# RWKV's chunk stage on 64x64 corners of TensorE, and heads in pairs in retention's scores and in the low-rank step

## The chip, the cores and the metric

The kernel runs on one core of a Trainium2 chip. The metric is device time in microseconds (us), the median of three runs. TensorE (PE in the profile) has two granted clocks, 1.2 and 2.4 GHz; the profile gives the granted clock as a share of the higher one.

## The reference, cut to what matters

A two-layer first block is followed by a second block of two layers with four attention variants, which the change does not touch. Each layer of the first block normalises `x` (256 tokens x 1024), projects it to retention, forgetting-attention and RWKV columns and to gates, runs the three branches (4 heads of 64 each), merges them and runs a gated FFN. The change is in three places: the RWKV recurrence, retention's scores, and RWKV's low-rank products.

```python
def step(state, ...):                       # one token, per head, state 64 x 64
    sa = jnp.einsum('bhvk,bhk->bhv', state, a_t)
    state = (state * w_t[:, :, None, :] + sa[..., None] * b_t[:, :, None, :]
             + v_t[..., None] * k_t[:, :, None, :])
    return state, jnp.einsum('bhvk,bhk->bhv', state, r_t)
...
w_pre = -jax.nn.softplus(-(w0 + jnp.tanh(xw) @ w2)) - 0.5    # xw: 64 columns
a = jax.nn.sigmoid(a0 + xa @ a2)                             # xa: 64 columns
g = jax.nn.sigmoid(xg) @ g2                                  # xg: 128 columns
```

The kernel computes the recurrence in chunks of 64 tokens. Within a chunk it needs the products of `a`, `r`, `b` and `k` of all token pairs, masked to the lower triangle, and the inverse of a unit triangular 64x64 matrix, which it builds in five doubling levels. From that follow each chunk's contribution to the state and to the output.

## The kernel before, in words

All matmuls write fp32 into eight PSUM banks of 128 partitions x 512. Banks 0 to 3 belong to the big projections, banks 4 to 7 to the branches. The weights of the projections come in pieces of 1 MB into a ring (SyncE's queue), ScalarE (ACT) makes a rounded high part (L1309), VectorE (DVE) the low part (L1710), and PE multiplies the parts in three fp32r passes.

PE's program is written out by hand (L1019 to L1107). From L1039 on, the gate columns are projected in 48 small units, `fill` (L649): each is 12 matmuls of 128x128 weights and 256 columns, all on line L659, and four of them make one group of 256 columns. The units stand between the pieces of the branches, so that PE has work while DVE or ACT handle a branch's last result. In the chunk stage (L1068 to L1102) the 256 tokens are two tiles `t` of 128 tokens, two chunks in each. Per tile PE runs:

- `rt_transposes` (L823): 16 transposes, of 64 columns each, so that head features lie in rows 0 to 63.
- `rt_matrices` (L846): per head, products over those 64 rows (L850, L851), 128 tokens by 256; then L855.
- levels v = 1 to 5: `rt_level_p` (L858), four 128x128 products (one a head, L865), then DVE's mask L2003; `rt_level_q` (L868), eight such products (L872, L873; only the four of L873 at v = 5), then DVE's two adds L2008 and L2009. One `fill` unit follows each P and each Q (none the last Q).
- `rt_ak_v` (L876, L878), `rt_solve` (L882, L886), `rt_chunk_terms` (L889: L892, L896, L901, L902), `rt_state` (L905: L912), `rt_output` (L916: L922, L923, L925, L926).

A 128x128 matrix of a tile holds the two 64x64 matrices of its chunks on its diagonal; the other half is masked to zero. An fp32 matmul leaves two records of each kind in the trace (two weight loads, two matmuls: I call them passes), an fp32r matmul or a transpose one.

DVE runs, in the levels of a tile, the masks and adds and between them whole jobs of 2048 columns in the table `slots`: a low part (L1710) or a scaling of gates (L1964). GpSimd copies chunk operands into zero-padded tiles (L2309, L2310) for L896, L901 and L902.

Retention (before the chunk stage) transposes q and k one head at a time (L682), ACT copies them, and `ret_scores` (L685) makes per head a product of 256 and one of 128 columns (L690, L691) over rows 0 to 63. The low-rank step transposes its 256 columns in three parts (L796 to L798) and multiplies by three weights (L806), two of them 64 rows high and both in rows 0 to 63.

Of the kernel before, what the change touches and what calls it, by code (L numbers as in the profile page):

```python
# [23 lines left out]
P = 128  # L24
D = 1024
KT = D // P
S = 256
# [42 lines left out]
def constant_tables():  # L70
# [15 lines left out]
    strict, incl = same * (j < i[None]), same * (j <= i[None])  # L86
    t["rmask"] = np.concatenate([strict, incl, strict, incl], 1)
    lev = []
    for l in range(LEVELS):
        s = 1 << l  # L90
        lev.append((j // (2 * s) == i[None] // (2 * s)) & (j // s % 2 == 1) & (i[None] // s % 2 == 0))
    t["lev0t"] = lev[0].T
# [81 lines left out]
def build(nc, x_in, w_in, w_fox, lora_w, p_all, w_out, w_gate_up, w_down, cols, vec1, mu, w_in2, w_out2,  # L174
          vec2, rpb, tables, out):
    with ExitStack() as ctx:
# [17 lines left out]
        lora = sb("lora", [P, 3, W4])  # L194
# [115 lines left out]
        ret_tp = sig("ret_tp", 4)  # L310
        ret_qk = sig("ret_qk", 4)
# [54 lines left out]
        rt_tp = sig("rt_tp", 8)  # L366
        rt_T = sig("rt_T", 8)
        rt_mat = sig("rt_mat", 8)
        rt_msk = sig("rt_msk", 8)
        rt_a = sig("rt_a", 2)  # L370
        rt_t0 = sig("rt_t0", 2)
# [8 lines left out]
        rt_zz = sig("rt_zz", 2)  # L380
        rt_vz = sig("rt_vz", 2)
        rt_rq = sig("rt_rq", 2)
        rt_rqc = sig("rt_rqc", 2)
        rt_g = sig("rt_g", 2)
        rt_gc = sig("rt_gc", 2)
# [3 lines left out]
        rt_sm = sig("rt_sm", 2)  # L389
        rt_y = sig("rt_y", 2)  # L390
# [49 lines left out]
        r_qk = carve(5120, 2048)[0]  # L440
        r_st, r_c = carve(0, 1536, 512)
        r_qkT = r_qk.rearrange("p (a h s) -> p a h s", a=2, h=NH)
# [12 lines left out]
        mats = scratch[:, 0:2048].rearrange("p (h c) -> p h c", h=NH)  # L455
        lo, w_ex, w_t1, w_t2 = carve(0, 512, 512, 512, 512)
        m_t, m_tt, m_p = (a.rearrange("p (h c) -> p h c", h=NH) for a in carve(2048, 512, 512, 512))
# [4 lines left out]
        m_g = carve(4096, 512)[0].rearrange("p (h c) -> p h c", h=NH)  # L462
        w_b = carve(4096, 512)[0]
        m_h = carve(4608, 512)[0].rearrange("p (h c v) -> p h c v", h=NH, c=2)
        w_kk = carve(4608, 512)[0]
        m_art = carve(5120, 1024)[0].rearrange("p (h c) -> p h c", h=NH)
        w_lT = carve(5120, 768)[0].rearrange("p (a s) -> p a s", a=3)
        m_bT, m_kT = (a.rearrange("p (h c) -> p h c", h=NH) for a in carve(6144, 512, 512))
# [4 lines left out]
        w_x = carve(8704, 1024)[0].rearrange("p (t h c) -> p t h c", t=NT, h=NH)  # L473
        w_bt, w_kt = carve(9728, 512, 512)
        m_s = carve(10752, 768)[0].rearrange("p (n h v) -> p n h v", n=3, h=NH)
        w_y, w_c2 = carve(11520, 512, 256)
        w_f3 = st[:, 424:488]
        w_fs = w_f3[:, 0:32].rearrange("p (n h c) -> p n h c", n=NT, h=NH)
        w_fe = w_f3[:, 32:44].rearrange("p (n h) -> p n h", n=3)

        kept = sb("kept", [P, 2560])
        m_zz, m_bz, m_vz = (kept[:, i * 512:(i + 1) * 512].rearrange("p (h c v) -> p h c v", h=NH, c=2) for i in range(3))
        m_rq = kept[0:HD, 1536:2560].rearrange("p (h c s) -> p h c s", h=NH, c=2)
# [32 lines left out]
        def _(sp):  # L516
# [16 lines left out]
            for l in range(DEPTH):  # L533
                ll = slice(l, l + 1)
                for n in range(len(IN_STARTS)):
# [4 lines left out]
                    if n == 3:  # L540
                        sp.dma_start(vec[:, 0:N_VEC1], vec1[ll].broadcast_to([P, N_VEC1])).then_inc(vec_in.sem, 16)
                        for i, k in enumerate((HD, HD, P)):
                            sp.dma_start(lora[0:k, i, :], lora_w[ll, i, 0:k, :].rearrange("o k n -> (o k) n"))\
                                .then_inc(lora_in.sem, 16)
                        sp.dma_start(w_mu, mu[ll].broadcast_to([P, 1024])).then_inc(mu_in.sem, 16)
# [48 lines left out]
        def _(pe):  # L594
# [77 lines left out]
            def ret_transposes(l):  # L672
# [5 lines left out]
                for a in range(2):  # L678
                    for t in range(NT):
                        for h in range(NH):  # L680
                            c = a * W4 + h * HD
                            last = tp(bank[4 + 2 * a + t][0:HD, h * P:(h + 1) * P], r_rot[:, t, c:c + HD], ident)  # L682
                        last.then_inc(ret_tp.sem, 1)

            def ret_scores(l):  # L685

                pe.wait_ge(*ret_qk.after(l, 4))
# [103 lines left out]
            def rw_lora_transposes(l):  # L791
                pe.wait_ge(*rl_s.after(l, 1))
                pe.sem_inc(passed.sem, 1)
                for t in range(NT):
                    s = lo[:, t * W4:(t + 1) * W4]
                    tp(bank[4][0:HD, t * P:(t + 1) * P], s[:, 0:HD], ident)  # L796
                    tp(bank[4][0:HD, S + t * P:S + (t + 1) * P], s[:, HD:2 * HD], ident)
# [3 lines left out]
            def rw_lora_products(l):  # L801
                pe.wait_ge(*rl_T.after(l, 1))
                pe.wait_ge(*lora_in.after(l, 3))
                for i, k in enumerate((HD, HD, P)):
                    for t in range(NT):
                        last = mm(bank[6 + i if i < 2 else 4][:, t * W4:(t + 1) * W4], w_lT[0:k, i, t * P:(t + 1) * P],  # L806
                                  lora[0:k, i, :], start=True, stop=True)
                    last.then_inc(rl_mm.sem, 1)

            def rw_decay_sums(l):  # L810
# [5 lines left out]
                for t in range(NT):  # L816
                    for h in range(NH):
                        c = (t * NH + h) * 4
                        last = mm(bank[6][0:HD, c:c + 4], w_lw[:, t * W4 + h * HD:t * W4 + (h + 1) * HD], tab["sel"],
                                  start=True, stop=True)  # L820
# [1586 lines left out]
```

## Time and profile before

| | |
|---|---|
| median of three runs (lowest to highest) | 1258.4 us (1252.48 to 1261.07) |
| the profiled execution: its time, its span | 1258.48 us, 1256.7 us |
| PE busy | 1223.0 us, 97% of the span |
| PE weight loads / DVE / ACT / GpSimd busy | 89% / 60% / 39% / 5% |
| mean granted clock | 0.99 |

A row of the timeline gives start, duration, engine, line, operation, tiles, shape and count. Shapes are rows*columns of the weights, then rows x columns of the moving operand. Matmuls overlap in their tails, so the cost of one to the engine is the distance from its start to the next start, not its duration; "x8" is eight records in a row of which the row gives the start of the first and the end of the last.

### The profile page before, as it was taken

To read this page: it belongs to the slowest core of one execution; us is meant where nothing else is said; L and a number is where in the kernel's file an instruction comes from. 1 tells how busy PE (TensorE), PEld (TensorE's weight loads), DVE (VectorE), ACT (ScalarE), POOL (GpSimd) and SP (SyncE) were. 2 spreads that over 40 slices of the span, in tenths; PEclk is the share of its full clock that TensorE was granted. 3 is DMA by queue.
4 is the path that set the end of the run, shared out by engine and by line. 5 is a ranking of instruction groups with operands and counts; after the bars stand their busy time and mean duration, and the time that the engine had idled before them with its cause. 6 is when DMAs were issued, how large, how long until landed. Compare 5 with 4: busy or idle time off the path is not lost. (4 is left out here: it accounts for less than half of the span.)

```text
span 1256.7 us, 19719 instructions
## 1 busy us (share of the span) xinstructions
PE 1223.0 (97%) x8388; PEld 1118.9 (89%) x8388; DVE 754.0 (60%) x942; ACT 495.8 (39%) x686; POOL 61.9 (5%) x67
## 2 busy tenths in 40 slices
PE   4999999999999999999999999999999999999997
PEld 3789999989999999789999989999999788887886
DVE  4486656465655556586647464655567765566654
ACT  3355412124333335355413113333335564455642
POOL 0002001000000000002001000000000300011000
PEclk9999999999999999999999999999999999999999
DMA  7643312425554445342222425544443534254320
GB/s 296 226 139 128 103 68 76 193 101 201 201 201 176 165 160 213 117 163 102 101 68 100 168 101 202 201 192 164 164 180 134 206 132 166 106 182 154 106 101 34
DMA packets 27458, 188.25 MB, mean 150 GB/s; under 512 B 3457, under 2 KB 4353, under 8 KB 5505
## 3 DMA queue, kind: packets, MB, share of 16 engines
q1 hardware_dynamic: 25808, 175.89, 37.9%
q10 hardware_dynamic: 1440, 8.55, 1.7%
q0 software_dynamic: 144, 2.89, 0.6%
q8 instruction: 48, 0.79, 0.3%
q14 instruction: 18, 0.14, 0.0%
HBM read 182.07 MB, written 5.24 MB: 149 GB/s over the span
## 5 line engine op out<-in xcount | busy, mean ns | idle before, releaser
L634 PE MATMUL bank<-in_low,h_high 128*128 128x512 f32 x352 | 139.7, 397 | 0.0
L634 PE MATMUL bank<-in_high,h_high 128*128 128x512 f32 x288 | 118.7, 412 | 19.3 <-DVE in_low L1710 18.6
L1710 DVE TENSOR_TENSOR in_low<-ring,in_high 128x2048 fp32r<-128x2048 f32 x48 | 109.9, 2295 | 34.4 <-ACT in_high L1309 34.4
L982 PE MATMUL bank<-h_high,gate_split 128*128 128x256 f32 x704 | 129.2, 281 | 0.2
L982 PE MATMUL bank<-h_high,up_split 128*128 128x256 f32 x704 | 128.8, 281 | 0.0
L1309 ACT ACTIVATE in_high<-ring 128x2048 fp32r<-128x2048 f32 x48 | 91.3, 1909 | 68.4 <-PE bank L634 68.0
L998 PE MATMUL bank<-act_split,down_split 128*128 128x256 f32 x960 | 118.2, 283 | 0.0
L998 PEld LDWEIGHTS bank<-act_split,down_split 128*128 128x128 f32 x960 | 116.4, 191 | 0.0
L659 PE MATMUL bank<-h_high,in_high 128*128 128x256 f32 x384 | 116.0, 302 | 0.5 <-DVE in_low L1710 0.5
L634 PE MATMUL bank<-in_high,x_low 128*128 128x512 f32 x288 | 114.3, 397 | 0.0
L982 PEld LDWEIGHTS bank<-h_high,gate_split 128*128 128x128 f32 x704 | 110.4, 189 | 0.9 <-DVE h_low L1661 0.6
L982 PEld LDWEIGHTS bank<-h_high,up_split 128*128 128x128 f32 x704 | 110.3, 189 | 0.0
L659 PE MATMUL bank<-x_low,in_high 128*128 128x256 f32 x384 | 109.4, 285 | 0.0
L659 PE MATMUL bank<-h_high,in_low 128*128 128x256 f32 x384 | 109.2, 284 | 0.0
L982 PE MATMUL bank<-h_low,up_split 128*128 128x256 f32 x352 | 99.4, 282 | 0.0
L982 PE MATMUL bank<-h_low,gate_split 128*128 128x256 f32 x352 | 99.3, 282 | 0.0
L634 PEld LDWEIGHTS bank<-in_high,h_high 128*128 128x128 f32 x288 | 55.3, 192 | 31.0 <-issue 18.9
L1483 ACT ACTIVATE gate_split<-ring 128x2048 fp32r<-128x2048 f32 x24 | 46.0, 1916 | 91.6 <-PE bank L982 72.5
L634 PEld LDWEIGHTS bank<-in_low,h_high 128*128 128x128 f32 x352 | 67.4, 192 | 13.6 <-issue 0.5
L659 PEld LDWEIGHTS bank<-h_high,in_high 128*128 128x128 f32 x384 | 74.5, 194 | 2.3 <-DVE in_low L1710 1.0
L1335 ACT ACTIVATE arena<-bank 128x512 f32<-128x512 f32 x24 | 14.3, 597 | 156.7 <-PE bank L659 156.7
L2082 DVE TENSOR_TENSOR down_split<-ring,down_split 128x2048 fp32r<-128x2048 f32 x20 | 45.8, 2292 | 49.8 <-ACT down_split L1483 49.8
(326 smaller groups left out, 2503.3 us busy)
## 6 DMA issues: line engine op xcount, KB each, us to landing
ring<-w_in_dram SPq DMA_DIRECT2D x72, 1024.0 KB, 4.8
ring<-w_gate_up_dram SPq DMA_DIRECT2D x44, 1024.0 KB, 7.4
ring<-w_down_dram SPq DMA_DIRECT2D x22, 1024.0 KB, 4.8
ring<-w_out_dram SPq DMA_DIRECT2D x16, 1024.0 KB, 5.8
ring<-p_all_dram SPq DMA_DIRECT2D x6, 1024.0 KB, 4.7
x_kept<-scratch ACTq DMA_DIRECT2D x4, 1024.0 KB, 4.2
x<-x_kept ACTq DMA_DIRECT2D x4, 1024.0 KB, 7.5
table<-tables_dram POOLq DMA_DIRECT2D x1, 2818.0 KB, 12.3
```

The costliest lines, as they stand in the source:

```text
L634: last = mm(bank[(n - n % 2 + t) % 4][:], a, b, start=c == 0 and i == 0, stop=c == KT - 1 and i == 2)
L659: last = mm(bank[g % 4][:, half * 256:(half + 1) * 256], a, b, start=k == 0 and i == 0, stop=k == KT - 1 and i == 2)
L982: last = mm(bank[2 * half + part][:, f * S:(f + 1) * S], a, b, start=k == 0 and i == 0, stop=k == KT - 1 and i == 2)
L998: last = mm(bank[4 + m // 2][:, m % 2 * S:(m % 2 + 1) * S], a, b, start=False, stop=end and m % 2 == 1 and k == 1 and i == 2)
L1309: f(in_high[n % 2][:], ring[:, n % 4, :].rearrange("p (k n) -> p k n", k=KT), ACT.Copy).then_inc(done.sem, 1)
L1335: f(gate[:, m:m + 2, :], b, ACT.Copy).then_inc(g_out.sem, 1)
L1483: f(w_split[part if pair is None else pair][:, 0, :], ring[:, 3 * half + part, :], ACT.Copy).then_inc(w_hi[part].sem, 1)
L1710: tt(in_low[n % 4][:], ring[:, n % 4, :].rearrange("p (k n) -> p k n", k=KT), in_high[n % 2][:].bitcast(F32), ALU.subtract).then_inc(low.s ...
L2082: tt(w[:, 1, :], ring[:, 3 * half + part, :], w[:, 0, :].bitcast(F32), ALU.subtract)\
```

## The change

**RWKV's chunk stage.** Each 128x128 product with two chunks on its diagonal becomes products of 64x64: weights in 64 rows and 64 columns of the array. `corners` = (0,0), (1,0), (0,1), (1,1) is the order in which the four quarters of the array are addressed; heads are transposed in pairs (128 columns at once), so that one head's features lie in rows 0 to 63 and the other's in 64 to 127. Row half and PSUM bank go together. P now handles both the triangular inverse and its transpose. GpSimd's copies and three of its tiles go. ACT takes over copies from PSUM (`m_h`, `w_y`, `m_at`). DVE's jobs in the levels are cut in halves and placed after P and after Q.

```diff
             def rt_level_p(l, t, v):
-                pe.wait_ge(*rt_t0.after(l, t + 1))
                 if v == 1:
-                    pe.wait_ge(*rt_msk.after(l, 4 * t + 4))
-                if v > 1:
+                    pe.wait_ge(*rt_msk.after(l, t + 1))
+                    pe.wait_ge(*rt_at.after(l, t + 1))
+                else:
                     pe.wait_ge(*rt_qc.after(l, 5 * t + v - 1))
-                for h in range(NH):
-                    last = mm(bank[5][:, h * P:(h + 1) * P], mats[:, h, S:S + P], m_t[:, h, :], start=True, stop=True)
+                for i in range(2):
+                    if v < LEVELS - 1:
+                        for o, c in corners:
+                            w = c ^ o
+                            mm(bank[6 + w][rows_of(c), i * HD:(i + 1) * HD], m_at[rows_of(w), o, 0, i], m_tt[rows_of(w), c, 0, i],
+                               start=True, stop=True)
+                    for o, c in corners:
+                        w = c ^ o
+                        last = mm(bank[6 + c][rows_of(w), P + i * HD:P + (i + 1) * HD], m_at[rows_of(c), o, 1, i],
+                                  m_tt[rows_of(c), w, 1, i], start=True, stop=True)
                 last.then_inc(rt_p.sem, 1)
...
-                for h in range(NH):
-                    mm(bank[4 + h][:, 0:S], m_kT[0:HD, h, :], m_art[0:HD, h, :], start=True, stop=True)
-                    mm(bank[4 + h][:, S:2 * S], m_bT[0:HD, h, :], m_art[0:HD, h, :], start=True, stop=True)\
-                        .then_inc(rt_mat.sem, 1)
...
+                for i in range(2):
+                    for o, c in corners:
+                        at = S + i * HD
+                        mm(bank[4 + o][rows_of(c ^ o), at:at + HD], a_(i, o, c), bk(0, i, o, c), start=True, stop=True)
+                for i in range(2):
+                    for o, c in corners:
+                        last = mm(wide(4, o, c, i * P), bk(0, i, o, c), ar(i, o, c), start=True, stop=True)
...
-                slots = ({1: lambda: gate_scale(l, 0), 2: lambda: in_split(l, 17, in_hi, in_lo), 4: lambda: in_split(l, 18, in_hi, in_lo)},
+                after_p = ({1: lambda: half_split(l, 16, 1), 2: lambda: half_split(l, 17, 0), 3: lambda: gate_scale(l, 0, 1),
+                            4: lambda: half_split(l, 18, 0)},
...
+                after_q = ({1: lambda: gate_scale(l, 0, 0), 2: lambda: half_split(l, 17, 1), 4: lambda: half_split(l, 18, 1)},
```

Over one tile: `rt_matrices` makes 24 products of 64 and 16 of 128 columns; P and Q make 16 products each at v = 1 to 4 and 8 each at v = 5; `rt_ak_v` 8; `rt_solve` 8 of 128 columns; `rt_chunk_terms` 16 of 64 and 8 of 128; `rt_output` 16 over the two diagonal corners and two or four of 128 rows; `rt_transposes` 8 full transposes.

**Retention and the low-rank step.** Transposes take two heads (or both 64-column parts) at once, and products over 64 rows alternate between the row halves:

```diff
-                for h in range(NH):
-                    q, k = r_qkT[0:HD, 0, h, :], r_qkT[0:HD, 1, h, :]
-                    mm(bank[4 + h][:, 0:S], k[:, 0:P], q, start=True, stop=True)
-                    mm(bank[4 + h][:, S:S + P], k[:, P:S], q[:, P:S], start=True, stop=True)\
-                        .then_inc(ret_sc.sem, 1)
+                for i in range(2):
+                    qk = [[r_qkT[rows_of(o), a, i, :] for a in range(2)] for o in range(2)]
+                    for o, (q, k) in enumerate(qk):
+                        mm(bank[4 + 2 * i + o][:, 0:S], k[:, 0:P], q, start=True, stop=True)
+                    for o, (q, k) in enumerate(qk):
+                        mm(bank[4 + 2 * i + o][:, S:S + P], k[:, P:S], q[:, P:S], start=True, stop=True)\
+                            .then_inc(ret_sc.sem, 1)
```

How PE's row moves at a level (v = 2 of the first tile), before; L865 is P, L659 a `fill` unit of twelve, L872 and L873 are Q:

```order
L865 MATMUL bank<-scratch 128x128 x4
L659 MATMUL bank<-h_high,in_high_53 128x256
L659 MATMUL bank<-x_low,in_high_53 128x256
...
L872 MATMUL bank<-scratch 128x128
L873 MATMUL bank<-scratch 128x128
L872 MATMUL bank<-scratch 128x128
L873 MATMUL bank<-scratch 128x128
```

The same place in the changed kernel, where L900 and L904 are P, L666 is the `fill` unit, and L914 and L918 are Q:

```order
L900 MATMUL bank<-scratch 64x64 x4
L904 MATMUL bank<-scratch 64x64 x4
L900 MATMUL bank<-scratch 64x64 x4
L904 MATMUL bank<-scratch 64x64 x4
L666 MATMUL bank<-h_high,in_high_53 128x256
L666 MATMUL bank<-x_low,in_high_53 128x256
...
L914 MATMUL bank<-scratch 64x64 x4
L918 MATMUL bank<-scratch 64x64 x4
L914 MATMUL bank<-scratch 64x64 x4
L918 MATMUL bank<-scratch 64x64 x4
```

P grows from 4 matmuls to 16, Q from 8 to 16, all of a quarter of the array; the unit between them stays. On DVE, the first level of the first tile before (L2003 the mask after P, L1964 a job, L2008 and L2009 the adds after Q):

```order
L1710 TENSOR_TENSOR in_low_55<-ring,in_high_52 128x2048
L2003 TENSOR_TENSOR scratch<-bank,table 128x512
L1964 TENSOR_TENSOR arena<-arena,root 128x2048
L2008 TENSOR_TENSOR scratch<-scratch,bank 128x512
L2009 TENSOR_TENSOR scratch<-scratch,bank 128x512
```

and in the changed kernel, where L2101 is the mask, L2107 the adds, L1785 and L2048 the halved jobs:

```order
L1785 TENSOR_TENSOR in_low_55<-ring,in_high_52 128x1024
L2101 TENSOR_TENSOR scratch<-bank,table 128x256 x2
L1785 TENSOR_TENSOR in_low_55<-ring,in_high_52 128x1024
L2107 TENSOR_TENSOR scratch<-scratch,bank 128x256 x2
L2048 TENSOR_TENSOR arena<-arena,root 128x1024
```

The mask is two operations of 256 columns for one of 512, the adds two of 256 for two of 512, and no job is longer than 1024 columns.

## Rows read from the trace of the kernel before

**Rows 1.** The page: busy us (share of the span) xinstructions; the clock in 40 slices.

```profile
PE 1223.0 (97%) x8388; PEld 1118.9 (89%) x8388; DVE 754.0 (60%) x942; ACT 495.8 (39%) x686; POOL 61.9 (5%) x67
PEclk9999999999999999999999999999999999999999
```

**Rows 2.** PE's waits, first layer's chunk stage: us in total, times, longest.

```profile
PE bank L835 <- DVE small L1732: 0.7, 1, 0.7
PE bank L865 <- DVE scratch L2009: 0.5, 2, 0.3
```

**Rows 3.** Timeline of PE, one level; start us, us, engine, line, tiles, shape, count.

```profile
161.90 1.13 PE L865 MATMUL bank<-scratch 128*128 128x128 f32 x8
162.79 0.36 PE L659 MATMUL bank<-h_high,in_high 128*128 128x256 f32 x1
...
164.30 0.38 PE L872 MATMUL bank<-scratch 128*128 128x128 f32 x2
...
166.00 0.37 PE L659 MATMUL bank<-h_high,in_high 128*128 128x256 f32 x1
...
167.71 1.13 PE L865 MATMUL bank<-scratch 128*128 128x128 f32 x8
```

**Rows 4.** Timeline of PE, `rt_matrices`.

```profile
142.23 0.70 PE L850 MATMUL bank<-scratch 64*128 64x256 f32 x2
142.77 0.59 PE L851 MATMUL bank<-scratch 64*128 64x256 f32 x2
...
145.79 1.05 PE L855 MATMUL bank<-scratch 64*128 64x128 f32 x8
146.77 0.39 PE L659 MATMUL bank<-h_high,in_high 128*128 128x256 f32 x1
146.99 0.28 PE L659 MATMUL bank<-x_low,in_high 128*128 128x256 f32 x1
```

**Rows 5.** Timeline of PE, `rt_output` and `rt_state` of the first tile.

```profile
186.74 0.33 PE L922 MATMUL bank<-scratch 128*128 128x64 f32 x2
...
190.43 0.67 PE L912 MATMUL bank<-scratch 64*64 64x64 f32 x8
191.03 0.39 PE L659 MATMUL bank<-h_high,in_high 128*128 128x256 f32 x1
```

**Rows 6.** Timeline of PE and weight loads, two attention heads in two row halves.

```profile
993.07 0.73 PEld L743 LDWEIGHTS bank<-scratch 64*128 64x128 f32 x8 [0.36 <-issue]
993.07 1.13 PE L743 MATMUL bank<-scratch 64*128 64x256 f32 x8
994.13 0.50 PE L634 MATMUL bank<-in_third,h_high 128*128 128x512 f32 x1
```

**Rows 7.** Timeline of PE, `rt_chunk_terms`.

```profile
181.56 1.09 PE L892 MATMUL bank<-scratch 128*64 128x128 f32 x8
...
185.20 0.39 PE L659 MATMUL bank<-h_high,in_high 128*128 128x256 f32 x1
```

**Rows 8.** Timeline of PE, retention's transposes and scores.

```profile
92.51 1.91 PE L682 MATMUL bank<-table,scratch 128*64 128x128 f32 x16
94.17 0.36 PE L622 MATMUL bank<-in_high,h_high 128*128 128x256 f32 x1
...
100.10 0.70 PE L690 MATMUL bank<-scratch 64*128 64x256 f32 x2
...
102.91 0.39 PE L659 MATMUL bank<-h_high,in_high 128*128 128x256 f32 x1
```

**Rows 9.** Timeline of DVE over the level of rows 3 and the one before.

```profile
157.86 2.28 DVE L1710 TENSOR_TENSOR in_low<-ring,in_high 128x2048 fp32r<-128x2048 f32 x1
160.47 0.69 DVE L2008 TENSOR_TENSOR scratch<-scratch,bank 128x512 f32<-128x512 f32 x1 [0.33 <-PE bank L873]
161.08 0.68 DVE L2009 TENSOR_TENSOR scratch<-scratch,bank 128x512 f32<-128x512 f32 x1
```

**Rows 10.** Stages by window: us, busy (x) of PE, PEld, DVE, ACT, POOL, granted clock, DMA, GB/s.

```profile
700.00:735.00 35.00, 35.00 (x213) 31.14 (x213) 17.39 (x30) 4.09 (x5) 1.20 (x2) 0.90 0.48 181
```

More of the change, by code:

```diff
@@ L839, in rt_transposes @@
[L839 to L856 removed]
+                    pe.wait_ge(*rt_yc.after(l, t))
@@ L905, in rt_state @@
+                last.then_inc(rt_h.sem, 1)
+                for i in range(2):
+                    for o, c in corners:
+                        last = mm(bank[6 + c][rows_of(o), i * P:(i + 1) * P].rearrange("p (a c) -> p a c", a=2),
+                                  m_tz[rows_of(c), 2 * i + o, 0:HD], m_bb[rows_of(c), t, :, i, o],
+                                  start=True, stop=True)
+                last.then_inc(rt_rq.sem, 1)
             def rt_state(l, n):
                 pe.wait_ge(*rt_s.after(l, n))
-                pe.wait_ge(*rt_gc.after(l, n // 2 + 1))
@@ new lines, in _ @@
+                    for o, c in corners:
+                        w = rows_of(c)
+                        tt(m_tt[w, c ^ o, 1], bk_ar[o][w, 0, :, 0], put(lev[0][w, 1], 1, 2), ALU.mult)
+                    fence()
+                    eight = m_tt.rearrange("p s a i c -> p (s a i) c")
+                    tt(eight, eight, put(id2, 1, 8), ALU.add)
+                    dve.wait_ge(*rt_at.after(l, t + 1))
+                    for o in range(2):
+                        tt(m_ka[:, o], bank[6 + o][:, S:2 * S].rearrange("p (i c) -> p i c", i=2), put(strict_incl, 1, 2), ALU.mult)
+                        last = tt(m_bb[:, t, 0, :, o], bk_ar[o][:, 0, :, 1], put(strict_incl[:, HD:P], 1, 2), ALU.mult)
@@ L1999, in _ @@
+                    last.then_inc(rt_msk.sem, 1)
                     if t == 0:
-                        in_split(l, 16, in_hi, in_lo)
+                        half_split(l, 16, 0)
                     for v in range(1, LEVELS):
+                        kinds = slice(0 if v < LEVELS - 1 else 1, 2)
+                        both = [[b[:, 0:S].rearrange("p (a i c) -> p a i c", a=2, i=2)[:, kinds] for b in bank[4 + n:6 + n]] for n in (2, 0)]
                         dve.wait_ge(*rt_p.after(l, 5 * t + v))
-                        tt(m_p, four(bank[5][:]), put(lev[v], 1, NH), ALU.mult).then_inc(rt_pc.sem, 1)
@@ L2015, in _ @@
-                    last.then_inc(rt_zz.sem, 1)
-                    if t == 1:
-                        merged(0)
+                        for s in range(2):
+                            last = tt(m_pr[:, s, kinds], both[0][s], put(lev[v][:, kinds], 2, 2), ALU.mult)
+                        last.then_inc(rt_pc.sem, 1)
+                        if v in after_p[t]:
+                            after_p[t][v]()
+                        dve.wait_ge(*rt_q.after(l, 5 * t + v))
+                        for s in range(2):
+                            last = tt(m_tt[:, s, kinds], m_tt[:, s, kinds], both[1][s], ALU.add)
@@ new lines, in _, with state @@
+                        last.then_inc(rt_qc.sem, 1)
+                        if v in after_q[t]:
+                            after_q[t][v]()
+                    if t == 0:
+                        in_split(l, 19, in_hi, in_lo)
+                    else:
+                        merged(0)
+                    def state(n, source):
+                        for o in range(2):
+                            w = rows_of(o)
+                            last = tt(m_s[w, n, :, w], source[w], put(w_fe[w, n], 2, HD), ALU.mult)
+                        last.then_inc(rt_s.sem, 1)
@@ L2018, in _ @@
+                    if t == 0:
+                        dve.wait_ge(*rt_hc.after(l, 1))
+                        dve.wait_ge(*rw_fe.after(l, 1))
+                        state(0, m_h[:, 0])
                     dve.wait_ge(*rt_rq.after(l, t + 1))
                     for c in range(2):
[L2020 to L2021 removed]
+                        src = bank[6 + c][:, 0:S].rearrange("p (i a c) -> p i a c", i=2, a=2)
+                        tt(m_rq[:, c], src[:, :, 0], m_art[:, :, 1, rows_of(c)], ALU.add)
+                        last = tt(m_g[:, c], src[:, :, 1], put(id2, 1, 2), ALU.add)
```

398 lines of the change are left out of this document (210 added, 188 removed).

## The prediction

> **What bounds the kernel now.** I read the page first: PE is busy 97% of the span, DVE 60%, ACT 39%, and the clock stands at its higher level almost throughout [rows 1]. So the end is set by what PE has to do. The waits of PE come next: in the first layer's chunk stage (122 us) it waits 0.7 us for DVE's sums of squares ahead of the second tile's transposes and 0.5 us for DVE's adds [rows 2]. Nothing else waits long enough to count. A change here is worth what it takes out of PE's own row, unless it makes another engine late.
>
> PE's timeline then gives the prices, from start to next start. A level takes 5.81 us (161.90 to 167.71) [rows 3]: P, eight passes, 0.89 us, or 0.111 a pass; a `fill` unit 1.51; Q, sixteen passes, 1.70; a second unit 1.71. The second unit is 0.2 longer than the first because DVE's second add starts at 161.08, takes 0.68, and only then may P begin, at 161.90 [rows 3, 9]. A unit without a wait is twelve passes of 0.119, 1.43 us.
>
> **Prices of the new forms.** L912 is a product of 64x64 weights and 64 columns, all in one corner: eight passes in 0.60 us, of which 0.13 go on entering and leaving, so 0.058 a pass, 0.117 a product [rows 5]. With 128 columns a pass is 0.109, a product 0.218, from L855 (0.98 us for eight, 0.11 of it leaving) [rows 4].
>
> Entering and leaving a form that uses only part of the array costs too: around `rt_matrices` the first pass pair takes 0.54 where the stream has 0.43, the last part 0.11 too long, and the first unit's pass 0.22 where 0.12 is usual: together over 0.3 [rows 4]. I take 0.34 us a visit for 64-column weights. A level had no such visit; it now has two.
>
> What the trace does not show is four corners at work together. From above it is bounded by L912: one after another, four products in 0.47 us. From below by the attention scores, which use two row halves: four fp32 products of 256 columns, eight passes, start at 993.07 and give way at 994.13, 1.06 us with both transitions, while L850 and L851 need 0.54 and 0.43 for each single product of that form, 1.8 for four [rows 4, 6]. The weight loads go along: eight of them within 0.73 us [rows 6]. So two halves cost what one does. If column halves behave alike, a round of four corners costs 0.117 us (64 columns) or 0.218 (128). If only row halves do, 0.234 and 0.436. I take the first: the nearest row shows parts of the array as independent, at no charge for the second.
>
> Here the Trainium skill speaks with two voices. TensorEngine Tiling (Key Properties) says that different tiles can execute weight loads and matmuls in parallel; TensorE: Matmul & The Clock Gate (Part 3, the mechanism) says that weight loads overlap with matmuls in flight only when the row group differs. The rows on row halves agree with both. By the first the sum is as below, by the second it is rival A.
>
> **The sum, per tile of 128 tokens (four in the kernel).**
> - Transposes: 16 narrow ones cost 1.66 us in the like stage of retention, and a visit [rows 8]; now 8 full ones at 0.111. Gain 1.1.
> - `rt_matrices`: 142.23 to 146.77, 4.54 us, and a visit of 0.4 [rows 4]. Now 24 products of 64 columns (6 rounds, 0.70), 16 of 128 (4 rounds, 0.87) and a visit, 1.91. Gain 3.0.
> - Levels 1 to 4: P and Q now have 16 products, 4 rounds, each: 0.47 + 0.34 = 0.81. The level becomes 0.81 + 1.43 + 0.81 + 1.43 = 4.48. Gain 1.33 each, 5.3. Level 5: P and Q, 0.89 each, and the wait of 0.2, become 2 rounds and a visit each, 1.14 together. Gain 0.8.
> - `rt_ak_v`, `rt_solve`: 16 passes of about 0.11, 1.7 us; now 0.23, and 0.44 with a visit. Gain 0.7.
> - `rt_chunk_terms`: 181.56 to 185.20 [rows 7], 3.64 and a visit; now 4 short rounds and 2 long, 0.91, and a visit. Gain 2.7.
> - `rt_output`: 186.74 to 190.43, 3.69 us for the first tile [rows 5], which with a fourth product a head makes about 4.6 for the second. Now 16 products over two corners (8 rounds of two, 0.94), two to four of 128 rows (0.44) and three changes of form inside at 0.2: 2.0 to 2.2. Mean gain 2.0.
>
> That is 15.7 a tile, 63 us for four. GpSimd's copies go, which was nobody's wait; `rt_state` stays at four products.
>
> **Retention and the low-rank step, per layer.** Retention's transposes gain 1.1 like the others. Its scores take 2.81 us (100.10 to 102.91) [rows 8]; in row pairs they take 2 x (0.43 + 0.22) = 1.3, gain 1.5: this is the form that the attention scores already show. Two of three low-rank products become a row pair, 8 passes of 0.216 in the time of 4, gain 0.9. Two of six transposes and a visit go, 0.5, and the decay sums lose a visit, 0.4. Together 4.4, 8.8 us for two layers. All of it lies on PE's row; the groups of 256 columns between give ACT and DVE the same cover as before.
>
> **What hides the rest, and what is late next.** DVE in a level: mask and adds become pairs of 256 columns. An operation of 512 takes 0.69 and one of 2048 2.28 [rows 9], about 1.04 ns a column and 0.16 fixed, so 0.42 for 256, and 0.76 for a pair, since starts follow before ends. With two half jobs of about 1.2 that is 3.9 us of a level of 4.48, and each answer (0.76 and 0.25 us of latency) fits the unit of 1.43 that covers it. That also ends the 0.2 us wait per level. At a level's start the eight small masks, the sum, and the four masks behind them are 3.5 us on DVE; PE has 0.9 of products and two units, 3.8. Thin, not negative. ACT's new copies: after the solve two of 512 columns (1.2 us), behind a high part of 1.9 in the first tile: a new wait of about 0.3; state and output add some 0.2. The wait of 0.7 ahead of the second tile goes, since the transposes now wait for ACT's copy of the output and no longer for the square sums. I charge 2 us in all for new waits; with every cover gone, that is 0.5 a level and 1 at each tail, it is 12, and if they cancel nothing.
>
> Sum: 1258.5 (profiled execution, 1.8 above its span, and equal to the median of 1258.4) - 63 - 8.8 + 2 = 1188.7. I forecast **1189 us**.
>
> **Rivals.**
> - *A: corners go two at a time.* For it: the trace shows concurrency for row halves alone. Against it: nothing in the trace runs two column halves. The tile has 48 short rounds and 8 long ones outside the output: 48 x 0.117 + 8 x 0.218 = 7.4 us more, 29 for four: **1218**.
> - *B, the slower side: corners go one at a time.* Whatever the cause, if the products start only at L912's pace [rows 5], each round costs three times more on top: 3 x 7.4 + 0.9 = 23 a tile, 92 in all: **1281**. P's 32 passes then cost 1.87 us where eight passes of the full array cost 0.89. The change loses from the point where a round takes more than 3.4 times 0.117, that is 0.4 us. Against it: the row pair, which alone would halve that.
> - *C: DVE or ACT sets the pace of the levels.* DVE would be at 87% of a level. If a half job lands in front of each answer, 0.4 us are lost in 16 levels and 1 us at four tails: **1199**. Against it: only if jobs start late, since the order puts each behind its answer.
> - *D: the clock falls.* In the window from 700 to 735, around the second layer's last outputs, the granted clock is 0.90 [rows 10]: 7 us at 1.2 GHz, which cost half of that. Just before, the array did narrow products with gaps (as in rows 5). Corners leave the array busy less, though the units of 1.43 us stay. If all chunk stages (some 160 us) ran at 1.2 GHz, the time would be about 1189 + 150 = **1340**; if such falls merely go, it is 4 us less.
>
> **How the numbers follow.** Forecast 0.60, A 0.20, C 0.10, B 0.05, D 0.03, the rest 0.02. The forecast's own spread is the visit: 76 visits or changes at 0.24 to 0.44 instead of 0.34 make 8 us either way. From 1180 that reaches up over C and A to 1222, and leaves out B, D and the edges, nearly 2 in 10. A measurement of this kernel can tell about 1% from no change. Faster by more than that are the forecast, A, C and part of the rest, 0.92; within 1%: 0.02; slower: B and most of D, 0.06.
>
> **What would show it right or wrong.** In the changed trace, P at levels 1 to 4 (L900 and L904) should take 0.8 us from its first start to the unit's, with 32 passes; 1.3 would be A, 2.2 B. A level should repeat every 4.5 us. PE should stay over 95% busy, with waits for DVE under 0.2 us in the levels and DVE near 70% in the chunk stage. The scores L698 and L700 should take 1.3 to 1.6 us. The chunk stage of a layer should be 32 us shorter. The forecast is wrong if a round of four corners costs much more than 0.12 us, if PE waits over 10 us in all for DVE or ACT, or if the clock row shows low stretches in the chunk stages.

## The result, and the profile after

The changed kernel takes 1196.2 us (median of 4 runs, 1193.46 to 1196.48). The kernel before took 1255.49 us beside it (4 runs, 1252.48 to 1261.07). The ratio is 0.9493, with a 95% interval of 0.946 to 0.9526: about 5% faster. The forecast was 1189 us, 7 us too low, with a range of 1180 to 1222. The profiled execution took 1196.37 us, with a span of 1194.3.

The page, against [rows 1]:

```profile
PE 1156.0 (97%) x9416; PEld 1048.2 (88%) x9416; DVE 730.2 (61%) x1002; ACT 501.3 (42%) x706; POOL 53.3 (4%) x47
```

PE has 1028 more matmuls and is busy for 67 us less; its share of the span is still 97%. So PE's row still sets the end. PE's timeline of the first tile's opening and first level, against [rows 3, 4] (start us, us, engine, line, tiles, shape, count):

```profile
138.63 0.46 PE L873 MATMUL bank<-scratch 64*64 64x64 f32 x16
138.91 0.62 PE L876 MATMUL bank<-scratch 64*64 64x128 f32 x16
...
140.36 0.39 PE L666 MATMUL bank<-h_high,in_high 128*128 128x256 f32 x1
...
143.59 0.34 PE L900 MATMUL bank<-scratch 64*64 64x64 f32 x8
143.76 0.30 PE L904 MATMUL bank<-scratch 64*64 64x64 f32 x8
143.87 0.30 PE L900 MATMUL bank<-scratch 64*64 64x64 f32 x8
143.99 0.30 PE L904 MATMUL bank<-scratch 64*64 64x64 f32 x8
144.22 0.38 PE L666 MATMUL bank<-h_high,in_high 128*128 128x256 f32 x1
...
148.14 0.34 PE L900 MATMUL bank<-scratch 64*64 64x64 f32 x8
```

`rt_matrices` takes 1.73 us where it took 4.54. P takes 0.63 (143.59 to 144.22), and inside it two rounds of four corners, eight passes each, take 0.23 (143.76 to 143.99), so one takes 0.117. The level repeats after 4.55 us (143.59 to 148.14), where it took 5.81. PE's waits over the whole kernel:

```profile
PE bank L641 <- DVE in_low L1793: 18.6, 1, 18.6
PE bank L900 <- DVE kept L2092: 5.6, 2, 2.8
...
PE bank L689 <- ACT small L1469: 1.3, 1, 1.3
```

The wait of 18.6 us is the program's start and stands in the trace of before with the same length. Two are new: 2.8 us in each layer, where the second tile's level 1 waits for DVE's masks (L2092), and 1.3 us in the second layer ahead of retention's transposes (L689). A lower clock comes with the first. By window (columns as in [rows 10]), the stretch with the wait and the one behind it (in the rest of the first layer's stage the clock is 1.00):

```profile
176.90:187.30 10.40, 7.62 (x149) 7.11 (x151) 8.04 (x19) 5.20 (x7) 1.21 (x2) 1.00 0.43 158
187.30:190.80 3.50, 3.50 (x44) 3.16 (x40) 0.76 (x2) 0.00 (x0) 0.00 (x0) 0.51 0.27 110
```

At 0.51 of full speed, the 1.2 GHz level, 3.5 us hold the work of 1.8. In the second layer the stretch is longer, and it sets in during the wait, which there ends at 625.19:

```profile
624.00:631.00 7.00, 5.81 (x80) 5.35 (x81) 2.58 (x9) 0.84 (x1) 0.00 (x0) 0.52 0.31 131
```

DVE shows why the masks are late:

```profile
178.91 0.42 DVE L2162 TENSOR_TENSOR scratch<-scratch,small 128x256 f32<-128x256 f32 x1 [1.58 <-POOL small L2381]
...
180.75 2.29 DVE L1793 TENSOR_TENSOR in_low<-ring,in_high 128x2048 fp32r<-128x2048 f32 x1
182.96 1.09 DVE L2081 TENSOR_TENSOR scratch<-bank,table 64x128 f32<-64x128 f32 x4
...
186.61 0.28 DVE L2092 TENSOR_TENSOR kept<-bank,table 128x128 f32<-128x128 f32 x1
```

The first masks' products were there at about 180. But ahead of the masks in DVE's queue stood a wait of 1.6 us for GpSimd's root, the four products that finish the first tile's output (1.8 us), and the split of group 20 (2.3 us). The masks ended at 186.9; the fill had covered PE until 184.2.

### The profile page after: what moved, and what is told of

The parts are those of the page before. It is cut to its first block and busy times, and to the rows that moved or that the text cites. A ratio compares the mean times of both kernels' runs of the same rounds, so it can differ in the third digit from the quotient of the medians.

```text
span 1194.3 us, 21803 instructions
## 1 busy us (share of the span) xinstructions
PE 1156.0 (97%) x9416; PEld 1048.2 (88%) x9416; DVE 730.2 (61%) x1002; ACT 501.3 (42%) x706; POOL 53.3 (4%) x47
## 5 line engine op out<-in xcount | busy, mean ns | idle before, releaser
L641 PE MATMUL bank<-in_high,h_high 128*128 128x512 f32 x288 | 118.9, 413 | 19.3 <-DVE in_low L1793 18.6
L666 PE MATMUL bank<-h_high,in_high 128*128 128x256 f32 x384 | 117.2, 305 | 0.5 <-DVE in_low L1793 0.5
L1793 DVE TENSOR_TENSOR in_low<-ring,in_high 128x2048 fp32r<-128x2048 f32 x38 | 86.7, 2287 | 37.7 <-ACT in_high L1369 37.7
L666 PE MATMUL bank<-x_low,in_high 128*128 128x256 f32 x384 | 109.6, 286 | 0.0
L666 PE MATMUL bank<-h_high,in_low 128*128 128x256 f32 x384 | 109.5, 285 | 0.0
L666 PEld LDWEIGHTS bank<-h_high,in_high 128*128 128x128 f32 x384 | 74.4, 194 | 5.8 <-issue 1.4
L666 PEld LDWEIGHTS bank<-x_low,in_high 128*128 128x128 f32 x384 | 74.7, 194 | 0.1
```

What stands on the lines that cost most here:

```text
L641: last = mm(bank[(n - n % 2 + t) % 4][:], a, b, start=c == 0 and i == 0, stop=c == KT - 1 and i == 2)
L666: last = mm(bank[g % 4][:, half * 256:(half + 1) * 256], a, b, start=k == 0 and i == 0, stop=k == KT - 1 and i == 2)
L1793: tt(in_low[n % 4][:], ring[:, n % 4, :].rearrange("p (k n) -> p k n", k=KT), in_high[n % 2][:].bitcast(F32), ALU.subtract).then_inc(low.s ...
```

## The experiments

Eight kernels ran, in two sets. Beside the result the kernel before had a median of 1255.49 us, beside the two sets 1258.52 and 1261.29, so differences of a us or two between sets are read from the traces, and not from the medians. **First, the new wait.** `norm_later` leaves every product on PE as it is and alters DVE's order between the tiles:

```
-                    if t == 1:
-                        in_split(l, 20, in_hi, in_lo)
                     dve.wait_ge(*rt_mat.after(l, 2 * t + 1))
...
+                    if t == 0:
+                        in_split(l, 20, in_hi, in_lo)
...
-                           {2: lambda: half_split(l, 21, 1), ...
+                           {1: lambda: finish(0, 0), 2: lambda: half_split(l, 21, 1), ...
...
+                            ... 4: lambda: finish(0, 1)})
```

`finish(0, ...)` is the wait for the root and two of the four products, then the other two.

> The changed kernel, but DVE's order between the two tiles of a layer is altered: the split of group 20 follows the first tile's sums of squares at once, then the second tile's masks, and the four products that finish the first tile's output move into free places of the second tile's levels (two behind P of level 1, two behind Q of level 4). Theory 1: the new wait of 2.8 us ahead of the second tile's level 1, twice, comes from DVE's queue (1.6 us of waiting for GpSimd's root, 2 us of products and 2.3 us of split stand ahead of the masks), and the falls of the clock right behind it (3.4 us in the first layer, 6.8 us in the second) come with the wait. Then the wait falls to at most 0.3 us, the two falls vanish, and the time is 1196.2 - 5.0 - (3.4 + 6.8)/2 = 1186 us. Rival: the falls come from the corners' lighter load and stay without the wait; then 1196.2 - 5.0 = 1191 us. Second rival: the products in the levels make new waits there, 0.5 us or more at level 1; then the time is above 1192 us.

Measured: 1186.23 us (6 runs, 1185.86 to 1186.7), ratio to before 0.9418 [0.9387, 0.945]. The wait is gone from the list, and the clock is at its full level in the stretch where it had fallen. DVE's split and masks, and PE's stretch:

```profile
177.10 2.29 DVE L1793 TENSOR_TENSOR in_low<-ring,in_high 128x2048 fp32r<-128x2048 f32 x1 [0.77 <-ACT in_high L1369]
179.31 1.09 DVE L2092 TENSOR_TENSOR scratch<-bank,table 64x128 f32<-64x128 f32 x4
...
182.96 0.28 DVE L2103 TENSOR_TENSOR kept<-bank,table 128x128 f32<-128x128 f32 x1
```

```profile
176.00:186.00 10.00, 9.87 (x198) 9.16 (x199) 7.86 (x19) 5.09 (x7) 1.20 (x2) 1.00 0.41 148
```

The masks end at 183.2, and P starts at 183.30, when its fill ends. The wait vanishes as theory 1 says, no fall of the clock is left in either chunk stage, and neither rival's time came. `split_first` moves the split alone:

```
                     if t == 1:
                         merged(3)
+                    else:
+                        in_split(l, 20, in_hi, in_lo)
                     dve.wait_ge(*rt_yrs.after(l, t + 1))
```

> The changed kernel with only the split of group 20 moved on DVE: it now stands ahead of the wait for GpSimd's root and of the four products, where before it stood behind them. It may start when ACT's high part is there (178.1 us in the trace of the first layer), so it covers the wait for the root; the masks then start at about 178.1 + 2.3 + 2.0 = 182.4 instead of 183.0 us. Theory 1 (DVE's queue makes the wait): the wait of 2.8 us becomes 2.2 us, twice, and the time 1195 us, or a little less if the falls of the clock become shorter with it. Rival (the wait is for ACT's copies or for the products themselves): no change of the wait. What it tells besides: whether a wait of about 2 us still has a fall of the clock behind it.

Measured: 1192.95 us (4 runs, 1192.77 to 1193.8).

```profile
PE bank L900 <- DVE kept L2090: 3.9, 2, 2.0
```

The wait shrank from 2.8 to 2.0 us, so it does depend on DVE's queue, and the time fell by 3.2 us, 2 more than expected. Its clock falls again behind the wait, but for a shorter time in the second layer (0.57 over the window from 624 to 628 us, and full again behind it), which is the other part of those 3.2 us.

**Second, how far corners are independent.** `corner_pairs` has the same products in another order, so that P alternates between two column halves of the same rows, and Q between two row halves of the same columns (P shown):

```
-                for i in range(2):
-                    if v < LEVELS - 1:
-                        for o, c in corners:
+                for w in range(2):
+                    for i in range(2):
+                        if v < LEVELS - 1:
+                            for c in range(2):
```

> The changed kernel; the same products, but P (L900 on) and Q issue them in another order. P: first all products of row half 0, alternating between the two column halves, then all of row half 1. Q: first all of column half 0, alternating between the two row halves, then all of column half 1. So at most two corners can be at work for most of the time: in P two column halves of the same rows, in Q two row halves of the same columns. Theory 1 (all four corners are independent, column halves as well as row halves): both take the same, eight rounds of two at 0.117 us and 0.16 for entering and leaving, 1.1 us instead of 0.625 (less some 0.1 if the second half starts while the first ends), and the time rises by 16 levels x 2 x 0.4 + 4 x 2 x 0.2 = 14 us: 1210 us. Rival A of the prediction (only different row halves overlap): P takes 16 x 0.117 + 0.16 = 2.0 us, Q 1.1 us.

Measured: 1203.28 us (2 runs). P, now on L900 and L903:

```profile
147.90 0.33 PE L900 MATMUL bank<-scratch 64*64 64x64 f32 x4
148.06 0.28 PE L903 MATMUL bank<-scratch 64*64 64x64 f32 x4
148.18 0.29 PE L900 MATMUL bank<-scratch 64*64 64x64 f32 x6
...
148.80 0.39 PE L666 MATMUL bank<-h_high,in_high 128*128 128x256 f32 x1
```

Four passes, one round of two column halves, take 0.12 us (148.06 to 148.18), as long as one product in one corner does alone: column halves overlap at no charge, as row halves do. P takes 0.90, and so does Q (150.43 to 151.34). Rival A's mechanism, overlap for row halves alone, is refuted. With it goes the second voice of the Trainium skill that the prediction quoted (TensorE: Matmul & The Clock Gate, Part 3, the mechanism): the rule that weight loads overlap only when the row group differs does not hold for these products. P is also 0.2 us faster than eight rounds and the two changes of form (1.10), and so the time rose by 7 us and not by 14: where the first half of P ends, products of the second already run (the row x6 has passes of both). That leads to the next run.

`corner_single` lets each corner do its four products in a row, and the solve its two corners one after the other:

```
-                for i in range(2):
-                    if v < LEVELS - 1:
-                        for o, c in corners:
+                for w, c in corners:
+                    for i in range(2):
+                        if v < LEVELS - 1:
```

> The changed kernel; P and Q issue all four products of one corner, then all of the next, and the solve (L939 on) the four of one diagonal corner, then of the other. Theory 1 (a product starts only when the one ahead of it in the queue has started, and waits for its corner): corners hardly overlap, P and Q take 16 x 0.117 + 0.16 = 2.0 us each, the solve 8 x 0.218 + 0.15 = 1.9 us; the time rises by 16 x 2 x 1.4 + 4 x 2 x 0.6 + 4 x 0.9 = 53 us: 1249 us. Theory 2, from the run with row halves in turn, where a product of the other half started as soon as it stood two behind the one that ran (the two low-rank products lost nothing, 1.07 us in both orders, and the scores 2.26 instead of 1.51): each corner starts two rounds behind the one before, P and Q take (4 + 3 x 2) x 0.117 + 0.16 = 1.3 us, the solve 6 x 0.218 + 0.15 = 1.5 us, and the time rises by 16 x 2 x 0.7 + 4 x 2 x 0.3 + 4 x 0.45 = 27 us: 1223 us.

Measured: 1225.26 us (2 runs), 29 above the changed kernel. P starts at 148.54 and gives way at 150.00, the solve takes 1.51:

```profile
148.54 0.32 PE L899 MATMUL bank<-scratch 64*64 64x64 f32 x2
148.70 0.28 PE L901 MATMUL bank<-scratch 64*64 64x64 f32 x2
148.82 0.33 PE L899 MATMUL bank<-scratch 64*64 64x64 f32 x4
...
150.00 0.39 PE L666 MATMUL bank<-h_high,in_high 128*128 128x256 f32 x1
```

```profile
171.60 1.58 PE L933 MATMUL bank<-scratch 64*64 64x128 f32 x16
173.11 0.39 PE L666 MATMUL bank<-h_high,in_high 128*128 128x256 f32 x1
```

The first two products, one corner's, run alone (x2, x2); from then on twice as many passes start in the same time (x4). That is theory 2, with P 0.14 us slower than its 1.33; theory 1 would have had 2.0. Four corners at once take 0.63 and one at a time would take 2.0, so in this order P has lost 0.83 of the 1.4 us that overlap gives. Rival B's price, one corner at a time, is not reached even here.

**Third, retention and the low-rank step.** `pairs_only` is the kernel before with this part of the change alone (transposes, scores, low-rank transposes and products, in the changed kernel's code).

> The kernel of before with only the second part of the change: retention's transposes and scores and the low-rank step by pairs of heads, the chunk stage as it was. The prediction's terms for these (transposes 1.1, scores 1.5, low-rank products 0.9, low-rank transposes 0.5 us a layer; the decay sums stay as before) give 4.0 us a layer, 8 us in all: 1255.5 - 8 = 1247.5 us against the median of before on the same chip, ratio 0.994. Rival: the saved time comes back as waits, since the groups of products behind it cover less of ACT's and DVE's work: ratio 0.998 to 1.000.

Measured: 1252.9 us (10 runs, 1250.85 to 1257.06) against 1258.52 for before (17 runs), ratio 0.9946 [0.9919, 0.9972]: 5.6 us instead of 8. The trace has a new wait:

```profile
PE bank L685 <- ACT small L1417: 1.0, 1, 1.0
```

In the changed kernel retention's transposes (L689) and scores (L698, L700) read, in PE's timeline:

```profile
91.96 1.07 PE L689 MATMUL bank<-table,scratch 128*128 128x128 f32 x8
92.78 0.36 PE L629 MATMUL bank<-in_high,h_high 128*128 128x256 f32 x1
...
98.69 0.70 PE L698 MATMUL bank<-scratch 64*128 64x256 f32 x4
99.23 0.39 PE L700 MATMUL bank<-scratch 64*128 64x128 f32 x4
...
100.20 0.39 PE L666 MATMUL bank<-h_high,in_high 128*128 128x256 f32 x1
```

Against before [rows 8] the scores gain 1.30 us (2.81 to 1.51) and the transposes 0.84 (1.66 to 0.82). In the low-rank products the gain is 0.85 (76.59 to 79.29 before, 77.00 to 78.85 now).

`halves_in_turn` is the changed kernel with the row pairs' order broken up:

```
-                    for o, (q, k) in enumerate(qk):
-                        mm(bank[4 + 2 * i + o][:, 0:S], k[:, 0:P], q, start=True, stop=True)
...
+                for o in range(2):
+                    for i in range(2):
```

> The changed kernel with the same products in retention's scores and in the first two low-rank products, but in another order: all products of the upper row half, then all of the lower, so that hardly two neighbours lie in different halves. If the gain there comes from two row halves at work together, L698 and the low-rank products lose it: the scores take 2.6 to 2.8 us instead of 1.5, the two low-rank products 1.9 instead of 1.1, so +2.0 us a layer, 4.0 us in all: 1200 us. Rival: the gain came from having fewer banks, signals or transposes to handle, and the order does nothing: 1196 us.

Measured: 1195.7 us (4 runs, 1193.52 to 1197.98): the time can't tell. The trace can. The low-rank products lose nothing (76.61 to 77.68, 1.07 us), the scores take 2.26:

```profile
98.31 0.70 PE L698 MATMUL bank<-scratch 64*128 64x256 f32 x2
98.84 0.38 PE L699 MATMUL bank<-scratch 64*128 64x128 f32 x2
99.06 0.70 PE L698 MATMUL bank<-scratch 64*128 64x256 f32 x4
99.50 0.49 PE L699 MATMUL bank<-scratch 64*128 64x128 f32 x4
...
100.57 0.39 PE L666 MATMUL bank<-h_high,in_high 128*128 128x256 f32 x1
```

In the code L698 and L699 alternate, one product of two passes each. Yet at 99.06 two products of L698 (x4) run together: the other half's first product started ahead of a product of L699 that stands before it in the queue. So the overlap is what gains, and part of it survives this order: the scores give back 0.75 of their 1.30 us. Half of the expectation failed: the two low-rank products, two a half, stand near enough to each other in any order. This profile also has the wait of 2.8 us twice, with no fall of the clock behind it (1.00 from 184 to 192 us and from 620 to 632). Nothing in the chunk stage was changed in it, so it tells what the wait costs without the clock, as used below.

**Fourth, DVE's jobs.** `whole_jobs` is `norm_later` with the splits of four groups (17, 18, 21, 22) whole again:

```
-                    ... 2: lambda: half_split(l, 17, 0), ... 4: lambda: half_split(l, 18, 0)
+                    ... 2: lambda: in_split(l, 17, in_hi, in_lo), ... 4: lambda: in_split(l, 18, in_hi, in_lo)
```

> The kernel with the norm's products moved (norm_later), but the splits of groups 17, 18, 21 and 22 are whole again (2.29 us in one place of a level instead of 1.22 in two). In the changed trace P's mask ends at 149.58 and Q's answer is wanted by the adds at 151.16, so a whole job runs until 151.87 and the adds until 152.6, and the next P is due at 152.65. Theory 1: each whole job costs 0.1 to 0.2 us of PE, eight of them 1 to 1.5 us: 1187.5 us. Rival (rival C of the prediction: DVE sets the pace once a job stands in front of an answer): 0.7 us each, 6 us: 1192 us.

Measured: 1185.71 us (4 runs, 1185.44 to 1186.11), no slower than the 1186.23 of `norm_later`. A whole job and the adds behind it:

```profile
149.90 2.28 DVE L1793 TENSOR_TENSOR in_low<-ring,in_high 128x2048 fp32r<-128x2048 f32 x1
152.10 0.75 DVE L2118 TENSOR_TENSOR scratch<-scratch,bank 128x256 f32<-128x256 f32 x2
```

The adds end at 152.85, and the next P starts at 152.97, when its unit is done. From the first tile's transposes to the second's PE takes 40.67 us, and 40.69 in `norm_later`. Neither the rival's 6 us nor my 1 us came: halving these four jobs buys nothing in the levels.

**Last, the second new wait.** `exp_early` is `norm_later` with ACT's two exponentials and its copy ahead of the wait for DVE's difference:

```
                 act.wait_ge(*rw_cum.after(l, 1))
-                act.wait_ge(*rw_cx.after(l, 1))
                 f(w_ep, bank[5][:], ACT.Exp)
                 f(w_em, bank[5][:], ACT.Exp, scale=-1.0)
-                f(w_ex, w_t1, ACT.Exp).then_inc(rw_ex.sem, 1)
                 act.wait_ge(*rw_fs.after(l, 1))
                 f(w_f3[:, 0:16], bank[6][:, 0:16], ACT.Copy).then_inc(rw_fc.sem, 1)
+                act.wait_ge(*rw_cx.after(l, 1))
+                f(w_ex, w_t1, ACT.Exp).then_inc(rw_ex.sem, 1)
...
+                dve.wait_ge(*rw_fc.after(l, 1))
                 tt(w_t1, bank[5][:], w_lw, ALU.subtract).then_inc(rw_cx.sem, 1)
```

> The kernel with the norm's products moved (norm_later), and on ACT the two exponentials of the decay sums and the copy of the chunk sums now stand ahead of the wait for DVE's difference, with DVE's difference waiting for them, so that only the third exponential stands behind it. In the second layer ACT sat until 527.0 us for that difference, then loaded a table (1.28 us) and did three exponentials and the copy, and PE waited 1.3 us for the copy ahead of retention's transposes. Theory: that wait is ACT's chain behind the difference, and goes whole: 1186.2 - 1.3 = 1184.9 us. Rival: DVE's chain itself (its difference ends at 526.9) is late next, and under 0.3 us are gained: 1186 us.

Measured: 1184.5 us (6 runs, 1183.84 to 1184.98), ratio to before 0.9395 [0.9363, 0.9427]. The wait at L689 is gone. In the changed kernel ACT's chain began at 527.00:

```profile
527.00 1.28 ACT L1465 ACT_TABLE_LOAD   x1 [3.37 <-DVE scratch L1981]
```

In `exp_early` the table is loaded at 517.87, during work that PE does anyway. Between the two layers' chunk stages PE takes 340.4 us, and 341.9 in `whole_jobs`, which has the wait; both traces are at the full clock there. So the wait is gone whole, and the rival, DVE's chain, is not late next. This is the fastest version, about 12 us below the change as made.

## Why the prediction was right

**The bound and the corner rounds: right.** PE's row set the end before and after. A round of four corners costs 0.117 us, as taken from one corner's pace, and the tile's stages came out near their terms. Rivals A (1218) and B (1281) needed another price, and `corner_pairs` shows that two column halves share that price too.

**The sum per tile: 15.2 and 15.5 us against 15.7.** From tile to tile of the first layer before and after, first transpose to first transpose (L835 and L842), the first tile took 194.84 - 138.96 = 55.9 us, and now 40.7:

```profile
138.96 0.27 PE L835 MATMUL bank<-table,scratch 128*64 128x128 f32 x1
...
194.84 0.27 PE L835 MATMUL bank<-table,scratch 128*64 128x128 f32 x1 [0.68 <-DVE small L1732]
```

```profile
136.23 0.27 PE L842 MATMUL bank<-table,scratch 128*128 128x128 f32 x1
...
163.96 0.64 PE L929 MATMUL bank<-arena,scratch 64*64 64x64 f32 x16
164.53 0.39 PE L666 MATMUL bank<-h_high,in_high 128*128 128x256 f32 x1
...
166.16 1.09 PE L939 MATMUL bank<-scratch 64*64 64x128 f32 x16
167.18 0.39 PE L666 MATMUL bank<-h_high,in_high 128*128 128x256 f32 x1
...
176.91 0.27 PE L842 MATMUL bank<-table,scratch 128*128 128x128 f32 x1
```

Term by term. Levels: 5.81 to about 4.53, gain 1.3, as forecast; two bursts of four rounds are 0.94, two units 2.86, so a visit is (4.53 - 3.80) / 2 = 0.36 against 0.34 taken, about half of it inside the unit behind. `rt_matrices`: 4.54 to 1.73, gain 2.8 (3.0). `rt_chunk_terms`: 3.64 to 1.07, gain 2.6 (2.7). **`rt_ak_v` and `rt_solve`: forecast 0.7, measured nothing.** They took 1.62 us and take 0.57 + 1.02 = 1.59. The step that failed is "now 0.23, and 0.44 with a visit": I counted two rounds of four corners for eight products. Row half and output half both follow the chunk there, so they use only the two diagonal corners, and eight products are four rounds of two: 4 x 0.117 and 4 x 0.218. `rt_output`, which I had counted by twos, came out right. `corner_single` backs this: with the two diagonal corners one after the other the solve takes 1.51.

**Retention and the low-rank step: forecast 8.8, gained 5 to 6.** The scores came out at 1.51, in the range named. The visits that go with the narrow forms were priced too high (the transposes gained 0.84 instead of 1.1), and in the second layer 1.3 us came back as a wait. "The groups of 256 columns between give ACT and DVE the same cover as before" was the failing step: the cover was the same, but the PE work that shrank had been part of it, and ACT must load a table there.

**New waits: forecast 2 us, measured 5.6 + 1.3, and the clock.** The step that failed is "Thin, not negative". It let DVE's masks start when their products are there. At the second tile DVE still has the wait for GpSimd's root, four products and a split ahead of them. It had the same queue in the kernel before, where it just fitted:

```profile
196.28 0.42 DVE L2063 TENSOR_TENSOR scratch<-scratch,small 128x256 f32<-128x256 f32 x1 [1.59 <-POOL small L2282]
...
205.16 0.68 DVE L1998 TENSOR_TENSOR scratch<-scratch,table 128x512 f32<-128x512 f32 x1
```

```profile
205.90 1.16 PE L865 MATMUL bank<-scratch 128*128 128x128 f32 x8
```

The last mask ended at 205.84 and P started at 205.90, 11.1 us after the tile's first transpose (194.84). In the changed kernel P is due 7.3 us after it (176.91 to 184.16): the 3.8 us that the change took out in between, in the transposes and `rt_matrices`, had been DVE's cover. Another 0.6 comes from the wait of 0.7 us that went [rows 2]: PE started 0.15 us behind the end of DVE's square sums and now starts 0.42 ahead of it. From there to the last mask DVE needs 9.6 us where it needed 11.2, which gives 1.6 back. Together that is the wait of 2.8.

What the wait and the clock cost is told apart by the second tile, from its first transpose to those of the last output (`y_transposes`, 230.99 in the changed kernel):

| | wait | low clock | first layer | second layer |
|---|---|---|---|---|
| changed kernel | 2.8 | 3.4 us, 6.8 us | 54.08 | 55.42 |
| `split_first` | 2.0 | 3.4 us, 3.4 us | 53.28 | 53.54 |
| `halves_in_turn` | 2.8 | none | 52.67 | 52.94 |
| `norm_later` | none | none | 50.00 | 50.26 |

So the wait costs 2.7 in each layer and the clock 1.4 and 2.5, 9.2 us in all. The profiled spans of the changed kernel and `norm_later` differ by 10.2, of which 1.0 lies ahead of the first tile. Without these 9.2 us and the 1.3 the changed kernel would be at some 1186 us, a little below the forecast.

The forecast of 1189 thus came within 7 us partly because its errors cancel. The gain per tile and the pairs were about 4 us too high, the waits 4.6 too low, and the clock behind them (3.9) was left out. Against that, the two falls of the second layer before are gone, which cost 5.4 us: its tiles take 58.00 and 68.82 us in that trace, where the first layer's take 55.88 and 65.54. The stated spread, the price of a visit, was not where the miss lay.

**The clock, rival D: half right.** The falls of before in its second layer, one of them near its last outputs [rows 10], are gone, as "if such falls merely go" had it, and corner work alone brought none: `norm_later`, `whole_jobs` and `exp_early` show none in either chunk stage. New falls came with the new wait. So one of the prediction's own signs of being wrong did show, low stretches in the chunk stages; the other two did not (a round cost 0.117, and the new waits are 6.9 us, under its 10). Its "waits for DVE under 0.2 us in the levels" failed too, at the second tile's level 1.

**Rival C: no.** DVE is busy 30.7 of 44 us from 140 to 184, the 70% forecast, and never sets the pace within the levels; it does at the tile's border.

The chunk stage is 94.8 us long instead of 121.4, so 26.7 us shorter and not 32. The first tile gives 15.2, the second 15.5 without the wait (65.54 to 50.00), less 2.7 of wait and 1.4 of clock.

## What to carry to other kernels

Small fp32 products on separate quarters of the array overlapped at no charge here, for row and column halves alike, as long as neighbours in the queue lie in different corners; going into and out of such a stretch cost 0.36 us. Count for each product group how many corners it really has, since block-diagonal ones have two. When you shorten a stretch of the engine that sets the pace, ask what other engines do behind it: what it loses in length they lose in cover, and a queue that just fitted becomes a wait. Then move what nobody waits for (here the end of a norm) behind what PE waits for next. A wait of 2.8 us in this PE-bound stretch cost 1.4 to 2.5 us more by the clock, where the clock fell.

## What was not expected of the hardware

PE starts products out of program order when they lie in another row half: in `halves_in_turn` the first product of the second row half stood behind the last one of the first half and started 0.43 us ahead of it (99.07, in the row that begins at 99.06, against 99.50). In `corner_single` each corner began while the one before had two of its four products left. A product thus overtook one other and not more, and four in a row on one part of the array cost time in both runs (0.75 us in the scores, 0.83 in P). The start order also means that the last product in the code need not be the last to end; no run here tested that.

The low clock comes in two ways. Beside a wait of PE of 2.0 or 2.8 us the profiles of the changed kernel, `split_first`, `corner_pairs` and `corner_single` show it at 1.2 GHz in both layers, that of `halves_in_turn` in neither, so the wait makes the fall likely but not certain. The kernel before falls without a wait: in its profile PE is busy all the time from 655 to 665 and from 720 to 730 us, at a granted clock of 0.66 in both. Beside `exp_early` its 11 runs go from 1254.12 us at a mean clock of 0.996 to 1266.33 at 0.983, the time following the clock, while the 6 of `exp_early` keep within 1.2 us at 0.996 to 0.997. What in the old kernel brings the falls was not tried. But it means that some 5 us of the gain are clock, and not instructions, by the 5.4 us of the profiled run.
